# A two-layer hybrid decoder step: where ScalarE splits weights, and where it empties PSUM, in the recurrence

## The reference: what is computed

```python
def _layer(x, ...):
    h = x + 0.5 * _rmsnorm(_swiglu(_rmsnorm(x, gains[0]), f1g, f1u, f1d), gains[1])
    m, ... = _mixer(_rmsnorm(h, gains[2]), ...)
    h = h + _rmsnorm(m, gains[3])
    h = h + 0.5 * _rmsnorm(_swiglu(_rmsnorm(h, gains[4]), f2g, f2u, f2d), gains[5])

def _mixer(xn, ...):
    u = xn @ w_in                      # 1024 -> 6672
    q, fr, iv, go, z, xbc, dt = split(u)
    # HGRN2, 8 heads of 128: S_t = diag(decay_t) S_{t-1} + k_t^T v_t, o_t = S_t^T q_t
    k = (1.0 - lb) * sigmoid(-fr);  decay from lb and sigmoid(fr)
    o_hg = _rmsnorm(o_hg, hg_norm_w) * silu(go)
    # Mamba-2, 16 heads of 64, on silu(causal_conv(xbc)), gated by silu(z)
    o = concatenate([o_hg, y]) @ w_out
```

## Time and profile before

| what | value |
|---|---|
| median of three runs | 1885.76 us |
| the profiled execution's own time | 1887.11 us |
| its span, first to last instruction | 1885.3 us |
| PE busy | 1779.5 us (94%) |
| DVE busy | 1028.7 us (55%) |
| ACT busy | 779.0 us (41%) |
| POOL busy | 252.3 us (13%) |
| share of PE in the chain that ended last | 86% |
| mean granted clock of PE | 0.979 of full speed |

### The profile page before, as it was taken

The page is one execution under the profiler, slowest core; times in us unless marked ns, Lnnn a source line. Parts: engine busy times, 40 slices in busy tenths (PEclk is TensorE's granted clock), DMA queues, the critical chain, the costliest instruction groups (busy, mean ns, idle before and its releaser), DMA issues.

```text
span 1885.3 us, 28831 instructions
## 1 busy us (share of the span) xinstructions
PE 1779.5 (94%) x12246; PEld 1673.4 (89%) x12246; DVE 1028.7 (55%) x1207; ACT 779.0 (41%) x912; POOL 252.3 (13%) x147
## 2 busy tenths in 40 slices
PE   6999989999998989999989999899899899899998
PEld 6999989888885789999989999798798758899997
DVE  5455355757685645444354443757485865554433
ACT  5444244332364544443344432542323644544323
POOL 0111000031113101110001110000303040011200
PEclk8999999999998999999999999999999989999999
DMA  4444434434353434444434444252434443344442
GB/s 144 156 150 141 155 109 132 131 118 123 96 156 120 142 112 134 156 138 151 152 97 154 142 148 156 91 178 82 129 112 129 151 118 126 102 156 155 139 152 73
DMA packets 237467, 250.12 MB, mean 133 GB/s; under 512 B 6920, under 2 KB 221648, under 8 KB 237382
## 3 DMA queue, kind: packets, MB, share of 16 engines
q1 hardware_dynamic: 199264, 230.18, 38.4%
q10 hardware_dynamic: 38118, 18.72, 3.6%
HBM read 228.36 MB, written 20.52 MB: 132 GB/s over the span
## 4 chain that ended last, share of the span: by engine, by line
PE 86%; ACT 5%; DVE 3%; DMA 3%; issue 1%; POOL 1%; SPq 0%; ACTq 0%; DVEq 0%; POOLq 0%
PE PS L1524 25%; PE PS L1526 25%; PE PS L1525 25%; PE PS L1621 3%; ACT WH L657 2%; DMA ssm_sample<-SIN 2%; PE PS L1545 2%; PE PS L1747 1%; DVE ACC L1261 1%; PE PS L1736 0%; DVE MS L1173 0%; DMA SIN<-state_ssm 0%; PE PS L1863 0%; PE PS L1591 0%; POOL WX L603 0%
## 5 line engine op out<-in xcount | busy, mean ns | idle before, releaser
L1044 DVE TENSOR_TENSOR WL<-RAW,WH 128x2048 fp32r<-128x2048 f32 x200 | 471.5, 2358 | 490.4 <-ACT WH L657 490.4
L1524 PE MATMUL PS<-XH,WH 128*128 128x320 f32 x2176 | 687.6, 316 | 26.4 <-ACT XB L657 6.7
L657 ACT ACTIVATE WH<-RAW 128x2048 fp32r<-128x2048 f32 x200 | 382.3, 1912 | 788.5 <-PE PS L1526 788.3
L1526 PE MATMUL PS<-XH,WL 128*128 128x320 f32 x2176 | 675.3, 310 | 0.0
L1525 PE MATMUL PS<-XL,WH 128*128 128x320 f32 x2176 | 675.3, 310 | 0.0
L1524 PEld LDWEIGHTS PS<-XH,WH 128*128 128x128 f32 x2176 | 411.4, 189 | 50.3 <-ACT XB L657 11.0
L1525 PEld LDWEIGHTS PS<-XL,WH 128*128 128x128 f32 x2176 | 411.6, 189 | 1.9 <-issue 0.8
L1526 PEld LDWEIGHTS PS<-XH,WL 128*128 128x128 f32 x2176 | 411.3, 189 | 0.0
L1524 PE MATMUL PS<-HH,WH 128*128 (+1 forms) x1024 | 320.3, 313 | 8.9 <-DVE HF L1202 3.9
L1525 PE MATMUL PS<-HL,WH 128*128 (+1 forms) x1024 | 317.0, 310 | 0.0
L1526 PE MATMUL PS<-HH,WL 128*128 (+1 forms) x1024 | 317.0, 310 | 0.0
(11 more groups left out here) (281 smaller groups left out, 1531.3 us busy)
## 6 DMA issues: line engine op xcount, KB each, us to landing
RAW<-w_in SPq DMA_DIRECT2D x52, 1024.0 KB, 5.3
RAW<-ffn_w_gate SPq DMA_DIRECT2D x44, 1024.0 KB, 5.3
RAW<-ffn_w_up SPq DMA_DIRECT2D x44, 1024.0 KB, 5.3
RAW<-ffn_w_down SPq DMA_DIRECT2D x44, 1024.0 KB, 4.9
RAW<-w_out SPq DMA_DIRECT2D x16, 1024.0 KB, 5.0
SIN<-state_ssm SPq DMA_DIRECT2D x16, 512.0 KB, 4.3
ssm_sample<-SIN SPq DMA_DIRECT2D x16, 512.0 KB, 4.6
SIN<-state_hgrn ACTq DMA_DIRECT2D x12, 512.0 KB, 5.8
```

Source lines behind the costliest of these rows:

```text
L657: return nc.scalar.activation(out, in_, ACT.Copy, scale=scale)
L1044: V.tensor_tensor(WL[:, slot, :], RAW[:, slot, :], WH[:, slot, :].bitcast(F32), ALU.subtract).then_inc(lo_ready.sem, 1)
L1524: pe.matmul(out, wh, hi, start=first, stop=False)
L1526: return pe.matmul(out, wl, hi, start=False, stop=last_)
```

## The change

In `projected` for group 1, in `conv_input` and in `gate`, ACT empties the finished unit's banks first, and then splits unit u + 2. For group 0 the order stays. ACT asks for two tables earlier: the one with sigmoid behind the first copies of `values(l, 0)`, and the one with silu behind the exponential that ends each group's norm. On DVE, the low parts at levels 3, 5 and 7 move from ahead of the `SUF` update to behind the pick, and the one behind the last pick moves behind the update of the prompt's state (`S2`).

```diff
@@ projected(l, g, c), ACT
             act.wait_ge(unit_done.sem, unit_done.after(l, u[1]) + 1)
-            split_hi(l, ahead(u))
+            if g == 0:
+                split_hi(l, ahead(u))
             b = 6 if g else 2 * (c % 4)
...
                 nc.scalar.activation(go[:, h], ps, ACT.Silu).then_inc(go_ready.sem, 1)
+            if g:
+                split_hi(l, ahead(u))
@@ hgrn(l, g), ACT
                 values(l, 0)
+                nc.scalar.preload_act_table_set("sigmoid_and_others")
...
             nc.scalar.activation(RTO[:], RTO[:], ACT.Exp, scale=-0.5).then_inc(orinv_ready.sem, 1)
+            nc.scalar.preload_act_table_set("silu_and_others")
@@ hgrn(l, g), DVE
-                if i > 2:
-                    beside(i - 2)
                 V.tensor_tensor(s1, s1, last(p2, m), ALU.mult).then_inc(tree_ready.sem, 1)
...
                 pick(l, g, i - 1)
+                if i > 2:
+                    beside(i - 2)
...
             pick(l, g, 7)
-            beside(7)
...
             q.then_inc(s2_ready.sem, 1)
+            beside(7)
```

## The result

| | before | after |
|---|---|---|
| median of 20 runs | 1890.72 us | 1883.76 us |
| lowest and highest | 1884.43, 1955.1 us | 1857.38, 1897.12 us |
| the profiled execution's own time | 1887.11 us | 1882.24 us |
| its span | 1885.3 us | 1880.4 us |
| PE busy | 1779.5 us | 1800.2 us |

The ratio of after to before is 0.9937, with an interval of 0.991 to 0.9963: 0.6% less time, where 1.4% was predicted, and outside the predicted range. Of the 20 runs after, 17 lie between 1876.9 and 1897.1, and three at 1857.38, 1860.12 and 1863.73, which is where the forecast of 1860 lay.

What follows compares the result with a forecast made beforehand. PE, busy 94% of the span, was taken to bound the kernel. The terms -24.0 - 3.1 + 1.0 = -26.1 us, from a median of 1885.76, gave 1860 us, with an 8-in-10 range of 1851 to 1870.

Steps and rivals of the forecast that it cites:

- Banks before the split: In the recurrence and gate unit 2, PE's five waits for ACT to empty banks 6 and 7 go: -24.0 us.
- The clock behind GO: Behind the wait for GO, PE's slower clock goes with the pause, 1.54 us once per layer: -3.1 us.
- Table loads: ACT's sigmoid and silu loads move earlier, replacing others, into covered time: cost 0, otherwise 1.28 us each.
- the later split: High and low parts come later by one emptying (0.7 us for one copy), inside another whole unit: cost 0.
- DVE's low parts behind the picks and S2: In the tree and behind S2, moved low parts don't delay PE: cost 0, with 1.8 us cover in the tightest stretch.
- Rival C: DVE becomes the bound and PE waits for W, up to 36.6 us: 1896 us; chance 0.04.
- B: At heads 1 and 3, YT is late after all: +5.6 us, 1865 us; chance 0.07.
- Heads 1 and 3: DVE's low part is ready 0.7 us later but ends as before, behind POOL: cost 0, otherwise +5.6 us.
- Gate unit 3, +1.0: Last gate unit: waits for Z and DEC cancel; BMK comes about 0.5 us later: +1.0 us for both layers.
- Rival A: In Mamba behind the last gate unit, the clock's falls move: +6.6 us (1866), or down to 1856 or 1850; chance 0.18.
- Rival D: Banks are not what PE waits for; the waits only change name, to the low part: 1880 us; chance 0.05.

Runs made afterwards that it cites:

- experiment 9: The changed kernel with POOL making BMK ahead of WXB, without the two early table loads: median 1849.31 us, ratio 0.9825.
- experiment 8: The changed kernel with POOL making BMK ahead of WXB, and DVE's low parts back at their places before the change: median 1845.25 us, ratio 0.9786.
- 7: The kernel before the change, with POOL making BMK ahead of WXB: median 1874.04 us, ratio 0.9919.
- experiment 3: The changed kernel, with POOL making BMK ahead of WXB: median 1849.72 us, ratio 0.9811.
- 4: The changed kernel with unread matmuls on PE, four ahead of the wait for DEC and five ahead of that for BMK: median 1847.99 us, ratio 0.9802.
- experiment 2: The kernel before the change, with Z ahead of the split in the last gate unit only: median 1899.95 us, ratio 1.0057.
- experiment 5: The changed kernel with four unread matmuls in the pause for DEC alone: median 1880.85 us, ratio 0.9887.
- experiment 6: The changed kernel with eight unread matmuls in Mamba's second pair of each layer: median 1868.38 us, ratio 0.9904.
- experiment 10: As experiment 3, with DEC ahead of the last gate unit's split on ACT and DVE's low part behind its first product of the pairs: median 1880.29 us.
- experiment 11: As experiment 10, with DVE's low part moved behind the first update of SIN: median 1883.8 us, ratio 0.9983.

## Why the prediction was wrong, point by point

- **Banks before the split, -24.0.** Right. The five waits are gone, and PE's idle time fell by 25.6.
- **The clock behind GO, -3.1.** Right. Without the pause of 3.02 the granted clock from 429 to 440 us is 1.00.
- **Table loads, the later split.** Right at 0. The early loads themselves turned out to be unneeded, though the sum counts 1.28 of GO's wait on them: without them PE does not wait for GO either (experiment 9).
- **DVE's low parts behind the picks and S2.** Right at 0: no line of PE waiting for W, KTOK or YT, and the part can be undone without loss (experiment 8). Rival C is out, B as well.
- **Heads 1 and 3.** Right at 0. The low part took 3.43 where 3.2 was forecast, and PE did not wait behind it.
- **Gate unit 3, +1.0. This is the step that failed.** Its waits went as written: Z 5.8 to 2.0, DEC 1.1 to 4.7, BMK 5.2 to 5.9 in both layers, together +0.5. But the step gave them a price in idle time alone, and let the sum of the first two be 0 because they add up to the same. The place was not one of equal pauses: 2.88 and 0.56 became 1.00 and 2.37, nearer to the pause for BMK, and what follows is eight pairs of small matmuls that can stay at 1.2 GHz once they start so. With the order of this one unit put back, the median is 1860.61, the forecast; with it, 1883.76. The term was +23 by the medians and +11 by the means, not +1.0, since it is a share of executions with a long stretch and not a fixed time.
- **Rival A** named the place and the cause, with 0.18, and mis-sized it. It let the clock fall at the pause for DEC and double 3.31 us per layer, or spare the fall at BMK. Both pauses saw a fall in the profiled execution. That behind DEC cost less than half of the 3.31 (1.4 us, worked out below). Its point against, 2.88 followed by the full clock, was of one execution too: in the profile of 7 the 10 instructions behind the same 2.88 took 2.37 instead of 1.28. That behind BMK was taken to end within a pair, since the earlier trace rows of one execution showed it so. In that row the end of the low stretch was an accident of one execution, and the bound should have been the whole of Mamba: 5.60 to 10.18 for each pair, up to 7 x 4.6 = 32 us per layer.
- **Rival D** is out: the waits didn't change name.

What the sum is worth without the long stretch, experiment 3 less 7 says: -24.3. By the terms it should be -24.0 - 3.1 - 0.2 (Z and DEC; BMK is early in both), and + 2.8 for the short fall behind DEC in both layers (from the wait for DEC on, the same instructions end after 564.71 - 560.00 = 4.71 us in 3 and 562.07 - 558.75 = 3.32 in 4): -24.5. The runs of either experiment spread over 5 to 6 us, so this bears out the sum and not each term.

Two things stay open. Why one execution has the long stretch and the next not: the same program gave 1857 and 1897, and behind pauses for BMK of 2.61 to 2.97 the two layers of one execution had low stretches of 61 and 7 us (after), 7 and 31 (experiment 2), 10 and 61 (experiment 5). And how much of its higher rate comes from the new pause for DEC, and how much from the 0.36 us by which the pause for BMK grew; experiments 2 and 5 had long stretches behind 2.61 too. The kernel before has runs near 1920, six of the 20, that are as far above its others as a long stretch would put them, but none of these was profiled.

## What to carry to other kernels

Price a moved wait by what PE does after it, as well as by its length: ahead of a phase of small matmuls, equal idle time in another place raised the median by 23 us here, and matmuls that nobody reads, put into the pauses, lowered it by 36. Where the rows of one execution show the clock falling and coming back, let the cost reach to the end of the phase in the range, since its return may be chance. And do the part of a change that has its own wait apart from the rest: here the gain lay in ACT's order in the recurrence, the loss in the same edit at one gate unit, and DVE's part and the table loads were worth nothing that the runs show.

## What the runs showed of the hardware

- TensorE can stay at 1.2 GHz while it is busy without a break: 0.50 from 573 to 633 us after the change, 48 us at 0.51 in experiment 5. Behind the same pause it was back within about 7 us in layer 1 after the change. With eight dense matmuls of 128x320 per layer in the pairs, six runs show no time as long as a long stretch makes it (1864.58 to 1869.86, experiment 6).
- The length of a pause doesn't decide alone: 2.37 was followed by a low clock in the profile after, and 2.36 by the full clock in experiment 2; 0.98 after 0.82 was enough in layer 0 of experiment 10, and waits of 1.0 at most in layer 1 of experiment 11.
- A DVE instruction with two inputs of 128x2048 ran beside POOL's two copies of 128x64, which took 2.09 instead of 0.41 us (experiments 10 and 3).
